# Output projection of a hybrid decoder layer: two unequal token passes, and the first up-projection pair prepared by quarters

## The reference, cut to what matters

```
h  = x + concat(o_g, o_d) @ w_out                       # output projection, residual
hn = rmsnorm(h) * ffn_norm_g
u, new_ffn = causal_dwconv(hn @ w_up, ffn_buf, w, b)    # w_up: 1024 x 5632 (gate | value)
y  = h + (silu(u[:, :2816]) * u[:, 2816:]) @ w_down
```

## Time and profile before

| what | value |
|---|---|
| median of 3 runs | 1624.13 us (1623.47 to 1630.41) |
| profiled execution, own time | 1628.96 us |
| its span, first to last instruction | 1627.4 us |
| PE busy | 1515.5 us, 93% |
| DVE busy | 1054.6 us, 65% |
| ACT busy | 638.4 us, 39% |
| POOL busy | 395.5 us, 24% |
| mean granted PE clock | 0.968 |

### The profile page before, as it was taken

The page is one execution under the profiler, slowest core; times in us unless marked ns, Lnnn a source line. Parts: engine busy times, 40 slices in busy tenths (PEclk is TensorE's granted clock), DMA queues, the critical chain, the costliest instruction groups (busy, mean ns, idle before and its releaser), DMA issues.

```text
span 1627.4 us, 30132 instructions
## 1 busy us (share of the span) xinstructions
PE 1515.5 (93%) x11911; PEld 1430.0 (88%) x11911; DVE 1054.6 (65%) x1575; ACT 638.4 (39%) x1102; POOL 395.5 (24%) x750
## 2 busy tenths in 40 slices
PE   7999999898688888788999799999999999999998
PEld 6999999898577777644898799999999999999998
DVE  7444389777557676456547988887878787534420
ACT  6434242332334443353423444444444445423222
POOL 4000166554432243153002322222222220000000
PEclk8999999999789999899899799999999999999999
DMA  6211111232112311185542122222222226745333
GB/s 220 97 48 52 28 47 35 87 100 92 31 37 54 105 25 38 46 328 156 193 148 93 53 78 79 71 78 72 77 80 79 82 92 207 262 159 198 132 107 108
DMA packets 177981, 165.63 MB, mean 102 GB/s; under 512 B 24245, under 2 KB 157163, under 8 KB 176184
## 3 DMA queue, kind: packets, MB, share of 16 engines
q1 hardware_dynamic: 173528, 154.30, 30.7%
q0 software_dynamic: 1664, 6.29, 1.0%
q10 hardware_dynamic: 2656, 3.21, 0.5%
HBM read 125.68 MB, written 37.96 MB: 101 GB/s over the span
## 4 chain that ended last, share of the span: by engine, by line
PE 47%; DVE 2%; issue 1%; DMA 1%; ACT 1%; SPq 0%; POOL 0%; ACTq 0%; DVEq 0%; POOLq 0%
PE f_pair L3498 27%; PE f_pair L3544 15%; PE f_pair L3452 3%; DMA w_raw<-in_w_out 1%; DVE feat L3194 0%; PE f_pair L3578 0%; ACT w_hi L2936 0%; DVE m_xP_lo L3208 0%; DMA up_raw<-in_w_up 0%; DVE feat L3213 0%; SPq L2800 0%; PE f_pair L3512 0%; PE f_pair L3421 0%; DVE feat L3160 0%; DVE w_lo L3152 0%
## 5 line engine op out<-in xcount | busy, mean ns | idle before, releaser
L3498 PE MATMUL f_pair<-m_xP_hi,up_w_hi 128*128 128x264 f32 x1232 | 254.6, 288 | 12.8 <-DVE m_xP_lo L3208 9.4
L3498 PE MATMUL f_pair<-m_xP_lo,up_w_hi 128*128 128x264 f32 x1232 | 252.5, 286 | 0.0
L3498 PE MATMUL f_pair<-m_xP_hi,up_w_lo 128*128 128x264 f32 x1232 | 252.3, 286 | 0.0
L195 PE MATMUL proj<-x_hi,win_hi 128*128 128x352 f32 x672 | 220.1, 327 | 0.0
L195 PE MATMUL proj<-x_hi,win_lo 128*128 128x352 f32 x672 | 217.3, 323 | 0.0
L195 PE MATMUL proj<-x_lo,win_hi 128*128 128x352 f32 x672 | 216.9, 323 | 0.0
L3498 PEld LDWEIGHTS f_pair<-m_xP_hi,up_w_hi 128*128 128x128 f32 x1232 | 192.9, 190 | 15.3 <-issue 10.2
L3498 PEld LDWEIGHTS f_pair<-m_xP_lo,up_w_hi 128*128 128x128 f32 x1232 | 193.0, 190 | 0.0
L3498 PEld LDWEIGHTS f_pair<-m_xP_hi,up_w_lo 128*128 128x128 f32 x1232 | 192.5, 190 | 0.0
L3544 PE MATMUL f_pair<-dn_g_hi,dn_w_hi 128*128 128x352 f32 x528 | 171.9, 325 | 0.2 <-DVE f_pre L3271 0.2
L3544 PE MATMUL f_pair<-dn_g_lo,dn_w_hi 128*128 128x352 f32 x528 | 169.7, 321 | 0.0
(11 more groups left out here) (462 smaller groups left out, 2932.3 us busy)
## 6 DMA issues: line engine op xcount, KB each, us to landing
dn_raw<-in_w_down SPq DMA_DIRECT2D x50, 512.0 KB, 4.0
up_raw<-in_w_up SPq DMA_DIRECT2D x44, 512.0 KB, 4.6
win_raw<-in_w_in SPq DMA_DIRECT2D x28, 512.0 KB, 3.9
g_scratch<-f_prod SPq DMA_DIRECT2D x22, 528.0 KB, 2.7
dn_g_in<-g_scratch SPq DMA_DIRECT2D x66, 176.0 KB, 3.6
p_key<-in_cache_k SPq DMA_DIRECT2D x32, 256.0 KB, 3.7
w_raw<-in_w_out SPq DMA_DIRECT2D x16, 512.0 KB, 6.1
x_scratch<-feat SPq DMA_DIRECT2D x1, 4224.0 KB, 12.0
```

The source lines that it names most:

```text
L195: mm = nc.tensor.matmul(out, w[:, k, :], x[:, k, g * TG:(g + 1) * TG], start=(k == 0 and i == 0), stop=(k == KT - 1 and i == 2))
L3498: mm = nc.tensor.matmul(pair[OF[name]][:, b, 0:HQ], w_[a][:, j, :], x_[t][:, j, b * HQ:(b + 1) * HQ], start=(name in FIRST_IN and j + x == ...
```

## The change

The 16 units become 8 units of 792 tokens (three PSUM banks each, two sets) and 8 units of 264 tokens (one bank each, out of four). The number and width of PE's matmuls in them stay the same: 576 and 192 of 264 columns. The head outputs are split into high and low parts in the same two widths, the 264-token rest one tile per unit. Weight tiles get five high/low buffers instead of two; the raw buffers stay two. In both loops `high(u + 2)` and `low(u + 2)` move to the front of the iteration, ahead of the square and the residual. The norm factors of the first 792 tokens are made after units 8 and 9, and eight scalings of 792 tokens run in iterations 10 to 13.

With tokens 0 to 791 normed after the first pass, the quarter pair (tokens 0 to 263, 528 to 791) is complete before the second pass is. So `difference`, `token_sums`, `last_sum`, `x_high` and `x_low` of P5, P6, P7, P4 and P3 are made in two pieces of 264 tokens (c = 0, c = 1), and PE takes these products of pair 0 piece by piece. `first_sums(0)` moves behind the last unit and the first quarter's token sums; `keep_u1(0)` moves behind the first four P5 casts.

The diff, cut to its core:

```diff
+    W_SLOT = [0, 1, 2, 0, 1, 2, 0, 1, 3, 4, 1, 2, 0, 3, 2, 1]
+    W_BEFORE = [max((v for v in range(u) if W_SLOT[v] == W_SLOT[u]), default=None) for u in range(NO)]
+    PASS = (slice(0, 3 * HQ), slice(3 * HQ, T))
+    BLOCKS = (slice(0, 3 * HQ // TB), slice(3 * HQ // TB, T // TB))
...
-    pair = [m.ps(f"f_pair{b}", [P, 2, 512]) for b in range(4)]
...
+    SPREAD = (banks[:, 3:6, 0:HQ], banks[:, 2:3, 0:HQ])
+    B_BANK = (0, 1, 6, 7)
+
+    def unit_banks(u):
+        if u < KT:
+            return banks[:, 3 * (u % 2):3 * (u % 2) + 3, 0:HQ]
+        b = B_BANK[u % 4]
+        return banks[:, b:b + 1, 0:HQ]
...
+            def difference(c_, j):
+                pool.wait_ge(scaled_h, KT * c_ + j + 1)
+                pool.wait_ge(o_lo_rest, KT - 1)
+                nc.gpsimd.tensor_tensor(t1[:, j, c_ * HQ:(c_ + 1) * HQ], hT[:, j, cols_of(1, c_)], hT[:, j, cols_of(0, c_)], sub
+                                        ).then_inc(t1_made, 1)
+
+            def last_sum(c_, j):
                 pool.wait_ge(x_lo_done["P2"], j + 1)
-                pool.wait_ge(t2_made, j + 1)
-                nc.gpsimd.tensor_tensor(hT[:, HK + j, one], hT[:, HK + j, one], hT[:, j, one], sub).then_inc(t4_made, 1)
+                pool.wait_ge(t2_made, HK * c_ + j + 1)
+                at = cols_of(0, c_)
+                nc.gpsimd.tensor_tensor(hT[:, HK + j, at], hT[:, HK + j, at], hT[:, j, at], sub).then_inc(t4_made, 1)
 
...
             def high(u):
-                s = u % 2
+                s, r = W_SLOT[u], u % 2
                 if u >= 2:
-                    act.wait_ge(loaded[s], 8 * (u - s))
-                    act.wait_ge(unit_done, u - 1)
-                nc.scalar.copy(w_hi[s][:, :, :], raw[s][:, :, :]).then_inc(split_hi, 1)
-
-            def o_high(t):
-                nc.scalar.copy(o_hi[:, t, :], head_out[t]).then_inc(o_hi_done, 1)
+                    act.wait_ge(loaded[r], 8 * (u - r))
+                if W_BEFORE[u] is not None:
+                    act.wait_ge(unit_done, W_BEFORE[u] + 1)
+                nc.scalar.copy(w_hi[s][:, :, :], raw[r][:, :, :]).then_inc(split_hi, 1)
...
@@ -2990,24 +3026,28 @@
                 nc.scalar.copy(wop[s % WR][0][:, :, :], W_OF[name]).then_inc(up_hi, 1)
 
             for t in range(1, KT):
-                o_high(t)
+                o_high(t, 0)
             high(1)
             nc.scalar.preload_act_table(ACT.Sqrt)
             for u in range(NO):
-                square_of(u)
                 if u + 2 < NO:
                     high(u + 2)
-                if u == KT:
+                if u == KT + 1:
                     roots(0)
-                if u in (10, 11):
-                    x_high("P1", 2 * (u - 10))
-                    x_high("P1", 2 * (u - 10) + 1)
                 if u in (12, 13):
-                    x_high("P2", 2 * (u - 12))
-                    x_high("P2", 2 * (u - 12) + 1)
-                if u == NO - 2:
+                    first_high("P1", 2 * (u - 12))
+                    first_high("P1", 2 * (u - 12) + 1)
+                if u == 14:
+                    first_high("P2", 0)
+                    first_high("P2", 1)
+                if u == NO - 1:
+                    first_high("P2", 2)
+                    first_high("P2", 3)
                     up_high(0)
                     up_high(1)
+                square_of(u)
+                if 1 <= u < KT:
+                    o_high(u, 1)
             for s in range(2, 5):
                 up_high(s)
...
 
+            def x_highs(name, c_):
+                for j in range(HK):
+                    x_high(name, c_, j)
+
+            x_highs("P5", 0)
             keep_u1(0)
-            for j in range(HK):
-                x_high("P5", j)
-            for j in range(HK):
-                x_high("P6", j)
-            for j in range(HK):
-                x_high("P7", j)
+            x_highs("P6", 0)
+            x_highs("P5", 1)
+            x_highs("P6", 1)
+            x_highs("P7", 0)
+            x_highs("P7", 1)
             nc.scalar.preload_act_table(ACT.Silu)
             up_high(5)
-            for j in range(HK):
-                x_high("P4", j)
+            x_highs("P4", 0)
...
@@ -3231,41 +3290,47 @@
                 nc.vector.tensor_tensor(lo[:, :, :], W_OF[order(s // NP)[s % NP]], r32(hi[:, :, :]), sub).then_inc(up_lo, 1)
 
             for t in range(1, KT):
-                o_low(t)
+                o_low(t, 0)
             low(1)
             for u in range(NO):
+                if u + 2 < NO:
+                    low(u + 2)
+                if u == KT + 1:
+                    inverse(0)
+                if KT + 1 < u <= KT + 5:
+                    scale(0, 2 * (u - KT - 2))
+                    scale(0, 2 * (u - KT - 2) + 1)
+                if u in (12, 13):
+                    first_low("P1", 2 * (u - 12))
+                    first_low("P1", 2 * (u - 12) + 1)
+                if u == 14:
+                    first_low("P2", 0)
+                    first_low("P2", 1)
+                if u == NO - 1:
+                    first_low("P2", 2)
+                    first_low("P2", 3)
+                    up_low(0)
+                    up_low(1)
                 residual(u)
                 gather(u)
-                if u + 2 < NO:
-                    low(u + 2)
+                if 1 <= u < KT:
+                    o_low(u, 1)
                 if u in ROWS_TURN:
                     keep_rows(ROWS_TURN.index(u))
-                if u == KT:
-                    inverse(0)
-                if KT < u <= KT + 4:
-                    scale(0, 2 * (u - KT - 1))
-                    scale(0, 2 * (u - KT - 1) + 1)
-                if u in (10, 11):
-                    x_low("P1", 2 * (u - 10))
-                    x_low("P1", 2 * (u - 10) + 1)
-                if u in (12, 13):
-                    x_low("P2", 2 * (u - 12))
-                    x_low("P2", 2 * (u - 12) + 1)
-                if u == NO - 2:
-                    up_low(0)
-                    up_low(1)
-                    first_sums(0)
+            for j in range(HK):
+                token_sums(0, j)
+            first_sums(0)
             for s in range(2, 5):
                 up_low(s)
             inverse(1)
-            for n in range(HK):
+            x_lows("P5", 0)
+            for n in range(KT):
                 scale(1, n)
+            x_lows("P6", 0)
             for j in range(HK):
-                x_low("P5", j)
-                scale(1, HK + j)
-                if j:
-                    token_sums(j - 1)
-            token_sums(HK - 1)
+                x_low("P5", 1, j)
+                token_sums(1, j)
+            x_lows("P6", 1)
 
...
                 pe.wait_ge(diag_made, x + 1)
-                if x:
-                    pe.wait_ge(scaled_h, KT)
-                for b in range(2):
-                    mm = nc.tensor.matmul(PW[:, b, :], c["ones"][0:TB, :], diag[:, 3 * b:3 * b + 3, :], start=True, stop=True)
+                pe.wait_ge(unit_kept, KT)
+                for b in range((BLOCKS[x].stop - BLOCKS[x].start) // 3):
+                    mm = nc.tensor.matmul(SPREAD[x][:, b, :], c["ones"][0:TB, :], diag[:, 3 * b:3 * b + 3, :], start=True, stop=True)
                 mm.then_inc(spread, 1)
 
             def unit(u):
-                s, half = u % 2, u // KT
+                s, out, at = W_SLOT[u], unit_banks(u), PASS[u // KT]
                 pe.wait_ge(split_lo, done(u))
-                if u >= 2:
+                if 2 <= u < KT:
                     pe.wait_ge(unit_kept, u - 1)
+                elif KT <= u < KT + 4:
+                    pe.wait_ge(unit_kept, KT - 1)
+                    if B_BANK[u % 4] >= 6:
+                        pe.wait_ge(rows_kept, 4)
+                elif u >= KT:
+                    pe.wait_ge(unit_kept, u - 3)
                 for k in range(KT):
```

More of the change, by code:

```diff
@@ L3158, in residual @@
                     dve.wait_ge(x_in[u], 16 * (KT - 1) if u else 16)
[L3159 to L3160 removed]
+                h = by_bank(hT[:, n, at])
+                nc.vector.tensor_tensor(h, unit_banks(u), h, add).then_inc(unit_kept, 1)
             def gather(u):
@@ L3168, in gather @@
                     dve.wait_ge(gathered, gathers(u) - 1)
-                nc.vector.tensor_tensor(total[:, half], total[:, half], square[:, :], add).then_inc(gathered, 1)
+                nc.vector.tensor_tensor(total[:, at], total[:, at], square[:, 0:at.stop - at.start], add).then_inc(gathered, 1)
             def keep_rows(q):
```

215 lines of the change are left out of this document (122 added, 93 removed).

## The result

| kernel | median, us (runs) | lowest to highest | profiled span |
|---|---|---|---|
| before | 1624.22 (9) | 1619.41 to 1630.74 | 1627.4 |
| changed | 1635.74 (9) | 1632.06 to 1638.25 | 1636.7 |

The ratio is 1.0054, with a 95% interval of 1.0037 to 1.0071: slower by 0.54%, 8.8 us by the ratio. Forecast were 1634.6 us and +10.5.

What follows compares the result with a forecast made beforehand. DVE was taken to bound the second pass and tail: T7 to P3 74.9 us plus 3.5 for POOL, 78.4, less 68.7 before, is +9.7; 0.8 of clock makes +10.5, 1634.6 us. Range +3 to +16, 1627 to 1640.

Steps and rivals of the forecast that it cites:

- T7: End of unit 7, the last 792-token unit; forecast at 851.5 us and used as zero for the later steps.
- S1 done: Behind the last unit, POOL's weight sum S1 (1.29 us) follows the moved first_sums and ends 45.0 us after T7.
- The first pass: Eight 792-token units: two start waits (0.71 and 1.18 us) go, 0.125 us per matmul, 27.0 us up to T7.
- DVE becomes the bound in the second pass: 264-token units: DVE iterations of 4.9 or 6.15 us beside PE units of 3.0; P1's matmuls late by 10 us.
- Seven iterations hold 1.35 us of waiting each: Second pass, argument against the third rival: DVE waits for square and high, 9 us by themselves.
- The moved sum and the moved copy: Behind the last unit: first_sums ends 43.7 us after T7, P1's copy on ACT 48.8; P2's first half waits for it.
- POOL: Eight last sums of 264 columns hold up DVE's SBUF instructions after the scalings; 3.5 us taken, bounds 0 and 5.2.
- The clock: Half of P2 and the spreading at the lower clock take 3.6 us; P7 partly at it adds 0.8.
- PE's idle time ahead of P1: PE idle some 6 us ahead of P1, waiting on up_low; a sign that the forecast is right.
- POOL and clock cost little: First rival: last sums fall in DVE's waits and P2 runs at full clock; +4.9, 1629.0 us; chance 0.26.
- The weight loads bind: Second-pass weight tiles land late through two raw buffers, 1 us in five iterations; +15, 1639 us; chance 0.08.
- The quarters keep PE fed: Third rival: P5 and P6 start early, DVE's own work 60.2 us; -8.5 and 1615.6 us with no wait; chance 0.06.

Runs made afterwards that it cites:

- e5: Changed kernel with high(u + 3) ahead of the square on ACT and the gather behind the low on DVE; stage 152.19 us against 154.54, ratio to before 1.0034.
- e1: Changed kernel with P1's copy (keep_u1) right behind the last square on ACT; stage 151.91 us against 154.54, 76.57 from T7.
- e2: Changed kernel with the weight sums (first_sums(0)) back beside the last unit, ahead of residual(15); stage 150.22 us against 154.54, 75.34 from T7.
- e4: Changed kernel with POOL's eight last sums cut from 264 to 8 columns; stage 150.43 us against 154.54, 75.43 from T7.
- e10: Kernel before the change with its four last sums moved from POOL to DVE and keep_u3 ahead of P4's lows; stage 145.78 us against 145.83, ratio 1.0007.
- e8: Changed kernel's unequal passes, but operands over halves of 528 tokens and P1's copy ahead of the P5 casts; stage 153.63 us against 154.54, ratio to before 1.0064.
- e6: Changed kernel with the edits of e1, e2 and e5 together; stage 148.14 us against 154.54, 72.79 from T7, ratio to before 1.0003.
- e7: e6 with the last sums made on DVE behind P7's lows instead of on POOL; stage 148.65 us against 148.14, ratio to before 1.0026.
- e9: e7 with the last sums behind the copy of P6's result and keep_u3 ahead of P4's lows; stage 147.49 us against 148.65, ratio to before 1.0014.

## Why the prediction was right, point by point

Times from T7, 850.6 in the trace (forecast 851.5):

| step | forecast | measured |
|---|---|---|
| residuals 10, 11, 12, 13 | 14.0, 18.9, 25.05, 31.2 | 13.6, 18.5, 24.7, 30.8 |
| residual(15) | 37.8 | 37.4 |
| token sums start | 39.05 | 38.6 |
| S1 done | 45.0 | 44.6 |
| copy of P1 done | 48.8 | 48.2 |
| P2's half and spread done | 52.4 | 52.2 |
| scalings done | 55.6 | 55.4 |
| P6's result copied | 66.5, with 3.5 of POOL 70.0 | 70.7 |
| P7's start to P3's start | 8.4 | 8.34 |
| P3 starts | 78.4, with 0.8 of clock 79.2 | 79.2 |

- **The first pass** is why the stage grew by 8.7 us and not by 10.5, though everything from T7 on took what was forecast. T7 stands 75.4 us behind the first matmul; the forecast's 851.5, set against the same start of before, is 77.1. The two waits went, as said, but the pace was mis-sized: the 144 matmuls of two 792-token units take 17.73 us, 0.123 each, where 0.125 was before. That is 1.2 of the 1.7 us; the rest is not traced.
- **DVE becomes the bound in the second pass:** right. The iterations are 4.90 and 6.13 us against 4.9 and 6.15, and PE waits where it was said to: unit 15, P1, P2.
- **Seven iterations hold 1.35 us of waiting each:** mis-sized. The two waits are 0.49 + 0.50 = 1.0 us, and only the residuals 9 to 12 have both behind them; behind residual 8 stand 1.43 us and behind the last three 0.49 each, 6.9 us in all and not 9. The 1.35 took in the add of the square, 0.35 us, which is DVE's own work inside that time; so the iteration's length was right and only the part called waiting was not. What could be had by handing over earlier was mis-sized further, and e5 measured it: 2.35 us.
- **The moved sum and the moved copy:** right as steps; from T7, e1 took 2.58 us back and e2 3.81. What the prediction did not say is that they are one wait: both together took 3.73.
- **POOL:** the mechanism was right, the size small. 3.5 us were taken between 0 and 5.2; the rows of e4 give 4.4. A sum of 264 columns takes POOL 0.8 us beside DVE and not half of S1's 1.29, and each costs DVE 0.55. By the Trainium skill (SBUF — State Buffer, section "SBUF: two separate sides") the port pair is held for the whole instruction. The trace agrees: DVE's 0.98 us starting at 911.18 end 0.28 us after POOL's sum (911.07 + 0.81), and are 0.43 without it.
- **The clock:** P2's half at the lower clock was right (2.98 + 0.89 = 3.87 us against 3.6). The 0.8 us for P7 was wrong: P7 took 3.17 us at the full clock. It made good what POOL was short of, 0.9 us, so the sum is nearer than its terms, and that is luck. One reading was loose: the 5.97 us that stand for the low clock are P6's, behind 3.83 us of idle time. P5, behind 2.71, was slow too (0.78 us for its first two matmuls), but e10's P3 ran at a granted clock of 1.00 behind 2.70 (0.48 for two). The length of the idle time alone doesn't tell which level follows.
- **PE's idle time ahead of P1** was 4.39 us, not some 6, since unit 15 was itself 2.54 us late.

Of the rivals, "POOL and clock cost little" is out: POOL alone costs DVE 4.4 us and the stage some 4. "The weight loads bind" did not happen: from 850 to 886 us ACT never waits for a load. It would have come next: in e5 a load is the reason of a wait of 3.81 us. "The quarters keep PE fed" has one true part: the quarters give 0.7 to 1.7 us (e8 against e1). It allowed DVE 8.5 us of standing still. From T7 to P3 DVE is idle for 13.1 of the 79.15 us and busy for 66.1, and of these 4.9 are stretching beside POOL (the 4.4 of e4's rows and 0.5 in the three weight lows). What is left, 61.2, is its own work, close to the rival's 60.2. So the rival fell on the waits and on POOL, 18.0 us where the prediction counted 19, and not on the amount of work.

The 2.3 us that e6 still owes can be read the same way. From T7 to P3, 72.8 us, DVE is idle for 5.7 and busy for 67.1; 6.7 of these are stretching beside POOL: 4.4 as in the changed kernel, 0.9 in two weight lows of the unit loop, 1.5 in the last add and the first token sum. Own work is 60.4 again. What stays open is how much of the 6.7 could be had: moving the last sums to DVE (e7, e9) exchanged one for the other, and no run takes the stretching away with the work left where it is.
